# Rows of x handed from block to block in halves of 128, w's low parts multiplied last, and the pair loops of two attention blocks reordered

## What is computed

```python
# two mixer layers (l = 0, 1)
mod = cs @ w_ada[l] + b_ada[l]                       # shift, scale, gate
h = rmsnorm(x, g_pre[l]) * (1.0 + scale) + shift
u = h @ w_in[l]                                      # 1024 -> 3864, then attention over 8 + 8 heads
x = x + gate * rmsnorm(y @ w_out[l], g_post[l])
# the four blocks after them
h = _rmsnorm(x) * (1 + scale) + shift
x = x + gate * block(h)                              # attention, ffn, latent attention, moe
```

## Time and profile before

| | |
|---|---|
| median of three runs | 1661.28 us (1660.46 to 1663.12) |
| profiled execution: its own time, its span | 1663.32 us, 1661.5 us |
| mean granted TensorE clock | 0.936 |
| PE busy | 1427.0 us, 86% |
| DVE busy | 1216.3 us, 73% |
| ACT busy | 862.0 us, 52% |
| layer 0, layer 1, na, ffn, mla | from about 49, 259, 471, 649, 886 us |

### The profile page before, as it was taken

How to read it: one execution, slowest core, us unless ns; L and a number is a source line. 1 busy time by engine, 2 the same in 40 slices (tenths; PEclk the granted TensorE clock), 3 DMA queues, 4 the chain that set the end, 5 groups by cost and what they waited for, 6 DMA issues and landing times.

```text
span 1661.5 us, 21232 instructions
## 1 busy us (share of the span) xinstructions
PE 1427.0 (86%) x7628; PEld 1191.2 (72%) x7628; DVE 1216.3 (73%) x1484; ACT 862.0 (52%) x1210; POOL 65.6 (4%) x82
## 2 busy tenths in 40 slices
PE   2799986999869976899986796999999999999993
PEld 1688676886758845899985685877777777777772
DVE  8667556866565655788785645789889888899895
ACT  0444444444434434233433554577777777776772
POOL 0000000000010000000000102100000000000001
PEclk9989898998989979899997897899999999999996
DMA  9764423735236632678774203699899999999782
GB/s 397 298 249 147 159 101 142 277 142 189 77 143 250 240 128 76 250 279 302 283 276 143 96 38 136 252 350 366 339 347 368 345 349 374 329 365 356 287 371 89
DMA packets 61537, 403.08 MB, mean 243 GB/s; under 512 B 6534, under 2 KB 9734, under 8 KB 15116
## 3 DMA queue, kind: packets, MB, share of 16 engines
q1 hardware_dynamic: 52416, 379.45, 60.3%
q10 hardware_dynamic: 7020, 15.17, 2.6%
q0 software_dynamic: 2016, 7.34, 1.2%
HBM read 393.01 MB, written 8.91 MB: 242 GB/s over the span
## 4 chain that ended last, share of the span: by engine, by line
PE 53%; DVE 27%; ACT 9%; issue 7%; DMA 2%; POOL 1%; ACTq 0%; DVEq 0%; SPq 0%; POOLq 0%
DVE w_lo L2177 16%; PE PS L826 14%; PE PS L828 13%; PE PS L827 13%; ACT w_hi L1602 4%; ACT xg L1696 2%; DVE acc L2194 2%; PE PS L998 1%; PE PS L978 1%; DMA raw<-in_ws 1%; DVE a_lo L2337 1%; DVE hb L2346 1%; DVE hb L2348 1%; PE PS L1251 1%; PE PS L896 1%
## 5 line engine op out<-in xcount | busy, mean ns | idle before, releaser
L2177 DVE TENSOR_TENSOR w_lo<-raw,w_hi 128x2048 fp32r<-128x2048 f32 x287 | 659.6, 2298 | 160.8 <-ACT w_hi L1602 138.3
L1602 ACT ACTIVATE w_hi<-raw 128x2048 fp32r<-128x2048 f32 x287 | 547.8, 1919 | 234.9 <-PE PS L828 222.2
L826 PE MATMUL PS<-w_hi,h_hi 128*128 128x512 f32 (+2 forms) x812 | 340.2, 419 | 28.6 <-DVE h_lo L2598 8.9
L827 PE MATMUL PS<-w_lo,h_hi 128*128 128x512 f32 (+2 forms) x812 | 321.3, 396 | 0.0
L828 PE MATMUL PS<-w_hi,h_lo 128*128 128x512 f32 (+2 forms) x812 | 321.2, 396 | 0.0
L826 PE MATMUL PS<-h_hi,w_hi 128*128 128x256 f32 x776 | 232.3, 299 | 21.4 <-DVE h_lo L2222 11.4
L827 PE MATMUL PS<-h_lo,w_hi 128*128 128x256 f32 x776 | 224.3, 289 | 0.0
L828 PE MATMUL PS<-h_hi,w_lo 128*128 128x256 f32 x776 | 224.1, 289 | 0.0
L826 PEld LDWEIGHTS PS<-w_hi,h_hi 128*128 128x128 f32 x812 | 157.9, 194 | 73.8 <-DVE w_lo L2177 15.7
L2194 DVE SCALAR_TENSOR_TENSOR acc<-raw,cs,acc 128x512 f32<-128x512 f32 x252 | 189.5, 752 | 8.9
L828 PEld LDWEIGHTS PS<-w_hi,h_lo 128*128 128x128 f32 x812 | 157.7, 194 | 33.7
(11 more groups left out here) (310 smaller groups left out, 1444.9 us busy)
## 6 DMA issues: line engine op xcount, KB each, us to landing
raw<-in_ws SPq DMA_DIRECT2D x359, 1024.0 KB, 5.6
y_rows<-ysb ACTq DMA_DIRECT2D x10, 512.0 KB, 7.4
rp<-in_rp ACTq DMA_DIRECT2D x8, 384.0 KB, 4.7
ckb<-in_ck ACTq DMA_DIRECT2D x2, 1024.0 KB, 4.9
y_rows<-ones ACTq DMA_DIRECT2D x3, 512.0 KB, 8.6
x<-in_x SPq DMA_DIRECT2D x1, 1024.0 KB, 11.6
gpost<-in_gpost ACTq DMA_DIRECT2D x2, 512.0 KB, 5.2
...
```

The lines of the kernel that those rows point to most:

```text
L826: t.matmul(out, lhs[0], rhs[0], start=start, stop=False, skip_group_check=True)
L827: t.matmul(out, lhs[0], rhs[1], start=False, stop=False, skip_group_check=True)
L1602: a.activation(wh[:, SPL_AT[e.phase][i], :], raw[:, r, :], ACT.Copy).then_inc(*e.inc("hi"))
L2177: v.tensor_tensor(wl[:, s, :], raw[:, r, :], wh[:, s, :].bitcast(F32), ALU.subtract).then_inc(*e.inc("raw_used"))
```

## The change

1. **Halves.** The norm of every block is made for m = 0 and then for m = 1: `turn(src, m)` makes eight transposes, `hb` is written in eight pieces of 128x128 per half (four by DVE, four by ACT), `h_hi` and `h_lo` in parts of (m, half of the columns). The update of x moved from the end of a block into the next one's `norm`, behind the first w_lo and `make_ab`. Where the block begins with a product of its own (`lay0`, `lay1`, `na`, `mla`) the new `first_sums` computes all of half m = 0 before it turns m = 1; `ffn` waits for all of h as before, now behind two turns. POOL makes one root for each half.
2. **w's low parts last.** In `first_sums` w_lo is waited for just before the four products that use it, and these come last in the second step.
3. **Layers.** Slot 0 is now `vm`, 512 columns of a product with rows as outputs. Four slots come before the loop, not three, so that `LAY_FILL` has 32 pieces in place of 40; `LAY_ADA` and the steps of ada in the stream move behind by a tick or two; `cmp_out` stands behind a piece and `turn_probs`. At the end, `turn_y(0, 1, 5)` stands inside `out_moba(0)`.
4. **na.** Two pieces come before `scores(0)`; all steps of ada stand between w's steps 2 to 13, where two of six came behind step 13; the output's pieces are reordered so that they can start at tick 9 rather than 10, and `turn_o(2)` is at tick 14.
5. **ffn.** The down products run over m outside k, and `ada(11)` stands before the last `down`, not behind.

The core of the diff:

```diff
-LAY_FILL = [(1, 2) if i % 4 == 3 and i < 16 else (1, 1) for i in range(18)] + [(0, 0)] * (LAY_TICKS - 18)
-LAY_ADA = {8: 2, 9: 3, 11: 4, 14: 5}
+LAY_FILL = [(1, 1)] * 14 + [(0, 1)] * 4 + [(0, 0)] * (LAY_TICKS - 18)
+LAY_ADA = {9: 2, 10: 3, 12: 4, 15: 5}
...
-NA_FILL = [(1, 2)] * 8 + [(0, 0)] * (NA_TICKS - 8)
-NA_OUT = {10: 1, 11: 1, 12: 1, 13: 1, 14: 1, 15: 1, 16: 2}
+NA_AHEAD = 2
+NA_FILL = [(1, 2)] * 6 + [(1, 1)] * 2 + [(0, 0)] * (NA_TICKS - 8)
+NA_OUT = {9: 1, 10: 1, 11: 1, 12: 1, 13: 1, 14: 1, 15: 2, 16: 2}
...
 def na_steps():
-    halves = dict(zip((2, 4, 5, 7, 8, 9, 10, 11), (x for j in range(4) for x in ada_steps(j))))
+    halves = dict(zip(range(2, 14), (x for j in range(6) for x in ada_steps(j))))
     out = []
-    for n in range(14):
+    for n in range(16):
         out.append(("w", n))
         if n in halves:
             out.append(halves[n])
-    return out + ada_steps(4) + ada_steps(5) + [("w", 14), ("w", 15)]
+    return out
...
-            def turn(src):
...
+            def first_sums(src, banks, width, m0_done=None):
+                for m in range(MT):
+                    turn(src, m)
...
+                    for kh in range(2):
+                        pe.wait_ge(*e.at("hi", kh + 1))
+                        pe.wait_ge(*e.at("h_hi", 2 * m + kh + 1))
+                        r = SPL_AT[e.phase][kh]
+                        sums = [(hh, wh), (hh, wl), (hl, wh)] if kh == 0 else [(hh, wh), (hl, wh), (hh, wl)]
+                        for i, (h_, w_) in enumerate(sums):
+                            if w_ is wl:
+                                pe.wait_ge(*e.at("raw_used", STEP_OF_SPLIT[e.phase][kh] + 1))
+                            if h_ is hl:
+                                pe.wait_ge(*e.at("h", 2 * m + kh + 1))
+                            for k in range(4):
+                                last = t.matmul(out, h_[:, 4 * kh + k, m * P:(m + 1) * P],
...
-                feat_slot(0, LAY_BANK[0:2], fresh=True)
+                first_sums(xn_l, LAY_BANK[0:2], 512)
                 feat_slot(2, LAY_BANK[2:4])
+                feat_slot(4, LAY_BANK[4:6])
                 ada(0)
-                tok_slot(4, LAY_BANK[4:6], 280)
+                tok_slot(6, LAY_BANK[6:8], 280)
...
-                    if i == 6:
-                        cmp_out(0)
-                    if i == 7:
-                        cmp_out(1)
...
                     if i < LAY_PAIRS:
                         turn_probs(i)
+                    if i in (6, 7):
+                        cmp_out(i - 6)
...
                 ada(FFN_SLOTS - 1)
+                ada(FFN_SLOTS)
                 down(FFN_SLOTS - 1)
-                ada(FFN_SLOTS)
...
+                updated(0)
+                if posted:
+                    normed(0)
+                    scaled(0)
+                    updated(1, (0,))
+                    lo(0, 0)
+                    updated(1, (1,))
+                    lo(0, 1)
+                    split_to(2)
+                    normed(1)
+                else:
+                    updated(1)
+                    normed(0)
+                    scaled(0)
+                    lo(0, 0)
+                    normed(1)
+                    lo(0, 1)
+                    split_to(2)
+                scaled(1)
+                lo(1, 0)
+                lo(1, 1)
+                split_to(SPL)
```

More of the change, by code:

```diff
@@ L98, in layer_steps @@
 def layer_steps():
-    halves = dict(zip((2, 3, 4, 5, 7, 8, 9, 10, 11, 12, 13, 14), (x for j in range(6) for x in ada_steps(j))))
+    halves = dict(zip((4, 5, 6, 7, 9, 10, 11, 12, 13, 14, 15, 16), (x for j in range(6) for x in ada_steps(j))))
     out = []
@@ L286 @@
     "rp_in3": {"na": 2},
-    "rstd": {"lay": 3, "na": 1, "ffn": 1, "mla": 3, "rt": 2, "end": 1},
+    "rstd": {"lay0": 2, "lay1": 4, "na": 4, "ffn": 2, "mla": 4, "rt": 2, "end": 1},
     "rwb": {"mla": 1},
@@ L755, in _ @@
             g.memset(nakz[:, 4:8], 0.0).then_inc(*e.inc("zeros_na"))
-            e.enter("ffn")
-            rstd(2, [(0, 2, D)])
-            e.enter("mla")
-            rstd(2, [(0, 2, D)])
+            for p in ("ffn", "mla"):
+                e.enter(p)
+                for m in range(MT):
+                    rstd(m + 1, [(m, m + 1, D)])
             for m in range(MT):
@@ L1009, in projections @@
                 def projections():
-                    for s in range(3, 8):
+                    for s in range(4, 8):
                         b = LAY_BANK[2 * s:2 * s + 2]
@@ L1313, in neighbourhood, with out_piece @@
-                pe.wait_ge(*e.at("xn", 2))
-                turn(xn_n)
-                tok_slot(0, LAY_BANK[0:2], 512, fresh=True)
+                def out_piece(half, m, c):
+                    w = arrived(12 + 2 * half + c)
+                    if half == 0:
+                        bank_free(2 * m + c)
+                    for k in range(4):
+                        kt = 4 * half + k
+                        lhs = [a[:, kt, m * P:(m + 1) * P] for a in (hh, hl)]
+                        last = mm3(PS[:, 2 * m + c, :], lhs, [a[:, k * 512:(k + 1) * 512] for a in w],
+                                   kt == 0, kt == KT - 1)
+                        if k == 3 and m == 1:
+                            last.then_inc(*e.inc("split_used"))
+                        if k == 3 and half == 1 and m == 0 and c == 1:
+                            last.then_inc(*e.inc("out_m0"))
+                        if k % 2 == 1:
+                            yield
@@ L1375, in _ @@
             used.clear()
-            pe.wait_ge(*e.at("xn", 2))
-            turn(xn_f)
+            for m in range(MT):
+                turn(xn_f, m)
             pe.wait_ge(*e.at("h", 4))
@@ L2012, in _ @@
             start("ffn")
-            squares(xn_f)
-            get_brow(4)
-            h_hi()
+            norm(xn_f, ahead=lambda: get_brow(4))
             ffn()
@@ L2152, in _ @@
             experts()
-            squares(xn_f)
+            for m in range(MT):
+                square(xn_f, m)
         @block.vector
```

485 lines of the change are left out of this document (229 added, 256 removed).

## The result

The changed kernel takes 1651.22 us (median of 9 runs, 1644.96 to 1657.31) against 1662.24 for the kernel before (9 runs, 1660.46 to 1664.24). The ratio is 0.9937, 95% interval 0.9920 to 0.9955: 0.6% faster. The forecast was 1626, range 1609 to 1645.

What follows compares the result with a forecast made beforehand. PE, busy 1427.0 of 1661.5 us, was taken as the bound, losing time at seams, single long waits and low clock. Terms summed to −43.5, with +8.5 for seam clock net −35: 1663.32 to 1628.3, as median 1626, range 1609 to 1645.

Steps and rivals of the forecast that it cites:

- 5.1 twice: Layers' pair loops: with shorter waits the clock stays up, 10.2 us of work at 0.51 taking 5.1, so −5.1 per layer.
- 6.0: na's loop: 12.73 us busy at clock 0.50 would take 6.4 at full clock; taken as −6.0.
- 8.5: Five split seams: a second idle stretch before m = 1, then work at the low clock; +8.5, bounds 0 and 16.
- −6.9: Seam into layer 1: slot 0 done at 280.5 instead of 287.4, −6.9.
- The same chain without the last two: Seam into na: layer 1's seam without the 0.7 wait for bank 3 and the 1.0 at low clock; −6.4.
- −3.4 all, −2 at worst: Layer's pair loop: the wait for `ce` goes under a piece and `turn_probs`; −3.4, at worst −2.
- −7.5: na's loop: waits of 6.9 for `acc` and 3.4 for `ptn` go, a new stall of about 2.8 appears; −7.5.
- −4.1: na: three output pieces of 1.36 each move from behind the loop into ticks that wait for the softmax; −4.1.
- −1.3: na: the last turn's h_lo (1.5) is covered by one more half of sums; −1.3.
- B: Rival: DVE stays busy in the loops, tick stalls and low clock stay; −19, 1642 us; chance 0.25.
- D: Rival, no change: the softmax chain of a tick, not PE, sets the loops' length; 1658 to 1664 us; chance 0.06.
- E: Rival, slower: the softmax chain sets the loops' length entirely, the loops give nothing; +6.6, 1668 us; chance 0.08.

Runs made afterwards that it cites:

- cmp_back: The changed kernel with cmp_out back in its old place behind the scores; ratio to the kernel before 0.9937 (0.9924 to 0.9950).
- ada_mixed: The changed kernel with only step 2 of ada a tick earlier in the layers (tick 8, not 9); ratio to the kernel before 0.9905 (0.9892 to 0.9917).
- na_split8: The changed kernel with eight low parts, not seven, made before na's first logits; ratio to the kernel before 0.9903 (0.9883 to 0.9924).
- na_ada6: The changed kernel with na's step 3 of ada in tick 6, not 7; ratio to the kernel before 0.9917 (0.9904 to 0.9930).
- ffn_back: The changed kernel with ada(11) behind the last down again in ffn; ratio to the kernel before 0.9963 (0.9949 to 0.9977).

## Why the prediction was wrong

The step that failed is the pair loops: waits were struck out of the sum as if DVE's queue in front of PE were empty, and other waits took their place, 16.0 us in a layer's loop where there were 13.8. By the prediction's own terms, without the clock (which it held apart as 5.1 twice, 6.0, 8.5 and 2.0 of the layers' starts):

- **Seams, right.** Into layer 1 the step −6.9, less the 1.65 of it that belongs to layer 0's end, and +0.7: −4.6. Measured −4.2. Into na −4.75 and −2.7: −7.45; measured −7.2. ("The same chain without the last two" is −6.9 and not the −6.4 that was written; with it the forecast is −7.95.) Start of layer 0 +1.5 (and 0.7); measured +1.0. The 0.7 for bank 3 had no wait of its own: PE waits 1.0 and 1.2 us there, 1.0 before. ffn's h 3.1 later: the first product came 20.1 us behind the sums and not 17.0, +3.1. POOL's second root was held as forecast (1.72 us, ending with w_lo; 0.19 without one).
- **A layer's loop, the step that failed.** "−3.4 all, −2 at worst" for the move of cmp_out, and −1.5 and −1.65, together −6.5 in a layer; measured +2.1 and +1.8, which is also what the waits of a loop rose by (13.8 to 16.0 and 16.2). I took a wait away from an instruction and looked behind it only for what that instruction delayed, not for what DVE had still to do. cmp_back shows that the 3.4 stand in DVE's queue, in front of whatever PE asks for next: 0 and not −3.4. And the shift of LAY_ADA, which I costed only by its `acc`, made the wait of 3.6 through DVE's buffer and bank 3; ada_mixed takes it out and gets 2.4 and 3.1 back. The two smaller terms came: `acc` 2.8 to 1.4, and one of three waits for h_lo. The new 1.6 for `ce` at the turn and 1.0 for `tmpo` have no run that takes them apart.
- **na's loop, right in sign, too large.** "−7.5", "−4.1" and "−1.3": −12.9; measured −4.5. The old waits of 3.4, 6.9, 1.5, 1.5 and 0.4 went, 13.7; new ones of 3.3, 3.6, 0.5 and 1.7 came, 9.1, where I had one of 2.8. The difference, 4.6, is all the loop gained. The 4.1 for output pieces laid into waiting ticks was counted twice, since the ticks' waits were already counted as gone (this is worked from the waits; no run moves these pieces back). na_split8 shows that the new 3.3 was a piece asked for before its low part, na_ada6 that the 3.6 comes back under other names.
- **The clock in the loops, wrong in size.** I wrote that the low stretches behind the long waits would vanish, −16.2. Busy time at the low clock in the three loops fell from 72.6 to 58.3 and 55.0, half of which is −7 to −9; the new wait of 3.6 us has a low stretch behind it too, as shown above. The 20.4 us at 0.50 in na are gone; two shorter stretches stand there (0.50 from 586.0 to 589.4 and from 596.2 to 599.6). Outside the loops it rose: seams +4.6, start of layer 0 +3.2, ffn +6.5, which is half of 14.3: +7. The forecast had +8.5 for that, near enough. The clock's sum is about nothing where −5.7 was written.
- **ffn and mla, right in the sum's sign only.** +6.5 foreseen, +2.4 measured: ffn took 2.9 more: its h came 3.1 later as forecast, but 1.0 of the 2.9 belongs to ada(11)'s new place (ffn_back). And this place before the last down, charged together with the third w_lo with 3.4, gains 4.9 over both blocks against the old one, once the update of x needs the gate early. With it in its old place the halves would have cost 1.9 in ffn and 5.4 in mla's start (ffn_back against before), near the forecast and for another reason.

Sum without the clock: about −29 forecast, −8.6 measured. Of the rivals none is it. B and D held parts of it (stalls stay), but it was neither the clock alone nor the softmax of every tick: a few single waits went and a few single waits came. The signs set for B, D and E didn't show (the mean clock is 0.936 to 0.940 in the two executions, and no tick after tick waits for `lgp` or `st`), and most of those for a right forecast did; none of them asked what would stand in place of a wait that goes. That na still made the kernel faster, while the layers as a whole gave nothing, was not foreseen: the forecast had 20.0 us from the layers' loops and 21.6 from na.

What stays open: whether the wait of 3.0 for `y` in tick 6 can be removed by another order of DVE's queue; what makes the new waits of 1.6 for `ce` and 1.0 for `tmpo`; why mla's start differs by 2 us where no edit reaches it; and why the layers' loops show 29.1 us of low work in one execution and 19.2 in another with the same waits to 0.1 us.
